# 32 of 256 tokens of an expert layer go by gathered rows on GpSimd and ScalarE instead of through the dense products

## The chip, the cores and the metric

One core of one Trainium2 chip. The metric is the device time of the kernel in microseconds (us), the median of several runs; lower is better.

## What is computed

A transformer layer of a hybrid kind on 256 tokens of width 1024, and then a second layer with other mixers, a cross attention and a feed-forward part. The change concerns the last part of the first layer, a lookup of experts:

```python
def peer_layer(h, w_q, keys, u, v):           # h: 256 tokens x 1024
    q = (h @ w_q).reshape(B, S, 8, 2, 128)
    ...
    # 8 heads x 16 = 128 experts (idx) and gates for each token, out of 16384
    def expert_block(args):
        ht, it, gt = args
        ue = jnp.take(u, it, axis=0)
        act = jax.nn.gelu(jnp.einsum('tkd,td->tk', ue, ht), approximate=False)
        ve = jnp.take(v, it, axis=0)
        return jnp.einsum('tk,tkd->td', gt * act, ve)
```

u and v are tables of 16384 rows of 1024 numbers, 64 MB each. All arithmetic is float32.

## The kernel before

The kernel doesn't gather. It multiplies every token with all 16384 rows of u, applies the gelu, multiplies the result by a gate that is zero for experts that the token didn't choose, and multiplies with all rows of v. Both tables are streamed once, as 128 units of 128x1024 floats each (512 KB), by the queue of SyncE (SP). The order of work is written out by hand for each engine; semaphores are the only link between them. The units of all weights of the kernel are numbered through, and the same steps are done for each unit i:

- SP: `fetch(i)` loads `raw[i % 4]` once the low part of unit i-4 is cut.
- ScalarE (ACT): `hi(i)` rounds the unit to float32r, `whi[i % 3]`, once TensorE (PE) has finished unit i-3.
- VectorE (DVE), or for some units GpSimd (POOL): `lo(i)` takes the rounded part from the raw one and so makes `wlo[i % 3]`. `on_pool` gives the choice: POOL for the first 62 or so units of u, DVE for the rest of u and all of v.
- PE: `three(...)` makes the product of both split operands in three float32r passes: high by high, high by low and low by high.

**Up-projection (u).** `lin_T`: for each unit 8 blocks of 128x128 weights, each with 3 matmuls whose moving operand is the 256 tokens of `hTh`/`hTl`: 24 matmuls of 128x256 for each unit. ACT evicts two units at a time with the gelu into `acts`, which holds 128 units by 256 tokens.

**Gates.** During the first 62 units DVE does the top-16 searches (`routing`) for both halves of the tokens. From unit 62 on, `gates` runs beside the units: for each group of 8 tokens and each half of the experts, DVE builds one-hot matrices (`oh`, `og_eq`, `og`, float16; three instructions with two operands in SBUF each), PE multiplies them (16 matmuls of 64 columns, L433 `bank<-og,oh`), and DVE multiplies the result into `acts` (`weigh`, L1715, one operand in PSUM). One group takes two steps, one step is made for each unit, and there are 64 groups: 33 of them during u and 31 during v.

**Down-projection (v).** For each unit, `cut_acts(n)` splits `acts` of the unit (ACT rounds, DVE subtracts), and PE makes 12 matmuls with 512 columns into four banks that are held for the whole of v. Later in v the norm of the `mem` input (`mem_norm`) and some loads of constants are put in.

`Side.step` moves the interleaved work on: each `yield` of a generator is one step.

Of the kernel before, what the change touches and what calls it, by code (L numbers as in the profile page):

```python
# [17 lines left out]
P = 128  # L18
# [15 lines left out]


# [28 lines left out]
    ("cfw", 66), ("cfb", 22),  # L64
# [53 lines left out]
def on_pool(i):  # L118

    slot = i - 2  # L120
    if BASE["u"] <= slot < BASE["u"] + 62:
# [34 lines left out]
own_act own_dve own_pool zeros x_sq hi_half lo_half lo_first f_xg f_xd f_act hd_mask  # L156
""".split()
# [39 lines left out]
def build(nc, x, mem, wdram, keep_d, con0_d, con1_d, con2_d, keys_d, w2c_d, gf_d, gf2_d, out):  # L197
    ctx = ExitStack()
    with ctx:
# [41 lines left out]
        s_raw = [sem(f"s_raw{i}") for i in range(NRAW)]  # L241
        s_in, s_in2, s_keep, s_con0, s_con1, s_con2, s_keys, s_w2c, s_gf, s_gf2, s_mem, s_out, s_w0, s_rest = (
# [103 lines left out]
        acts = t3(A2[:, :], P)  # L346
# [11 lines left out]
        assert 8192 + at0 + 2048 <= 256 * 61 and 8192 + at0 + 4096 <= 256 * 72  # L358
# [63 lines left out]
        def pe_program(e):  # L422
# [136 lines left out]
            def lin_T(u0, units, src, K, first=None, after=None, steps=(1,)):  # L559
# [215 lines left out]
            def gates(half):  # L775
                o1 = t4(oh1[:, :], OP, P)
                o2 = og[:, :].rearrange("p (m j i r) -> p m j i r", m=OP, j=2, r=2)
                for g in range(T // OB):
                    G = 32 * half + g
# [263 lines left out]
            lin_T(BASE["u"], 62, hTv, KD, steps=U1_STEPS)  # L1043
            side.drain()
            side.lists[0] += [gates(0), gates(1)]
            lin_T(BASE["u"] + 62, 66, hTv, KD)

            for i in range(4):
                use(i)
            for n in range(128):  # L1050
# [6 lines left out]
                for m in both:  # L1057
                    e.wait_ge(s["ca_lo"], m + 1)

# [19 lines left out]
                if n == 72:  # L1079
                    side.lists[0].append(mem_norm())  # L1080
# [67 lines left out]
        def act_program(e):  # L1148
# [176 lines left out]
            def cut_acts(n):  # L1325
                if n > 127:
                    return
                e.wait_ge(s["g_mul"], 32 if n < 64 else 64)
                if n >= 2:
                    e.wait_ge(s["w"], BASE["v"] + max(n - 7, 0))  # L1330
                act(cut(0, n), acts[:, n, :], ACT.Copy).then_inc(s["ca_hi"], 1)

            def mem_norm():
                e.wait_ge(s_mem, 32)
                e.wait_ge(s["ca_lo"], 72)
# [232 lines left out]
            def gelu(n0):  # L1568
                def f(n, pb):
                    if 256 * (n0 + n + 2) > 15872:  # L1570
                        e.wait_ge(s["rt_dve"], 8)
                    act(acts[:, n0 + n:n0 + n + 2, :], pb, ACT.Gelu).then_inc(s["ev_act"], 1)
# [5 lines left out]
            def first_cuts(u):  # L1578
                if u == 64:
                    cut_acts(0)  # L1580
                    cut_acts(1)

            lin_T(BASE["u"] + 62, 66, gelu(62), first_cuts)
            for n in range(128):
                hi(BASE["v"] + n + 2)
                if n == 62:
# [5 lines left out]
                if n == 72:  # L1592
# [105 lines left out]
        def dve_program(e):  # L1698
# [297 lines left out]
            def routing(b):  # L1996
# [62 lines left out]
                tt(g2[:, :, 1, :], gt, g2[:, :, 0, :], ALU.subtract).then_inc(s["rt_dve"], 1)  # L2059
                yield  # L2060

            def gates(half):
# [6 lines left out]
                def build(g):  # L2069
                    G, t = 32 * half + g, g * OB  # L2070
# [15 lines left out]
                def weigh(g):  # L2086
                    G, t = 32 * half + g, g * OB
# [6 lines left out]
                for g in range(T // OB):  # L2094
# [5 lines left out]
                weigh(T // OB - 1)  # L2100

            def cut_acts(n):
# [3 lines left out]
                tt(cut(1, n), acts[:, n, :], cut(0, n).bitcast(F32), ALU.subtract).then_inc(s["ca_lo"], 1)  # L2106
# [346 lines left out]
            lin_T(BASE["u"], 62, steps=U1_STEPS)  # L2453
            side.drain()
            side.lists[0] += [gates(0), gates(1)]
            lin_T(BASE["u"] + 62, 66)
            cut_acts(0)
            cut_acts(1)
            for n in range(128):
                lo(BASE["v"] + n + 2)  # L2460
                if n == 62:
                    side.drain()
                cut_acts(n + 2)
# [3 lines left out]
                if n == 72:  # L2467
# [79 lines left out]
        def pool_program(e):  # L2547
# [14 lines left out]

            def units(u0, n, steps=(1,)):
                for i in range(u0, u0 + n):
                    lo(i + 2)
                    side.step(steps[(i + 1) % len(steps)])
# [20 lines left out]
            own(e.memset(mhalf, -0.5))  # L2587
# [266 lines left out]
```

## Time and profile before

| what | value |
|---|---|
| device time, median of 3 runs (lowest, highest) | 1445.22 us (1444.06, 1445.54) |
| span of the profiled execution | 1441.8 us |
| own time of the profiled execution | not listed apart; the median of the runs is 3.4 us above the span |
| busy: PE, DVE, ACT, POOL | 99%, 67%, 51%, 15% of the span |
| TensorE's granted clock | full, in all 40 slices of the page |

How to read it: PE is the matmuls, PEld the loads of weights beside them, L433 is the line in which the helper `mm` emits each matmul, L1154, L1712 and L1715 are the helpers `act`, `tt` and `stt` of ACT and DVE. So an instruction is known by its tiles, not by its line. POOL is idle in most of the kernel and busy in the first half of u.

### The profile page before, as it was taken

To read this page: it belongs to the slowest core of one execution; us is meant where nothing else is said; L and a number is where in the kernel's file an instruction comes from. 1 tells how busy PE (TensorE), PEld (TensorE's weight loads), DVE (VectorE), ACT (ScalarE), POOL (GpSimd) and SP (SyncE) were. 2 spreads that over 40 slices of the span, in tenths; PEclk is the share of its full clock that TensorE was granted. 3 is DMA by queue.
4 is the path that set the end of the run, shared out by engine and by line. 5 is a ranking of instruction groups with operands and counts; after the bars stand their busy time and mean duration, and the time that the engine had idled before them with its cause. 6 is when DMAs were issued, how large, how long until landed. Compare 5 with 4: busy or idle time off the path is not lost.

```text
span 1441.8 us, 25221 instructions
## 1 busy us (share of the span) xinstructions
PE 1422.6 (99%) x10281; PEld 1290.2 (89%) x10281; DVE 967.4 (67%) x1752; ACT 738.5 (51%) x1066; POOL 212.7 (15%) x122
## 2 busy tenths in 40 slices
PE   8999999999999999999999999999999999999997
PEld 7989989999999999998777778888899788899986
DVE  5565674693944777778888876655577864677754
ACT  5674654545454444444444445544567754655543
POOL 5000000488883000000000000000114100000000
PEclk9999999999999999999999999999999999999999
DMA  6433456455555545445545466555543453455552
GB/s 241 142 132 125 138 157 216 141 186 180 187 180 182 170 162 174 164 164 173 174 164 174 164 222 245 181 185 188 175 147 118 159 177 112 154 188 185 181 190 103
DMA packets 67219, 245.07 MB, mean 170 GB/s; under 512 B 7456, under 2 KB 7712, under 8 KB 66848
## 3 DMA queue, kind: packets, MB, share of 16 engines
q1 hardware_dynamic: 66960, 243.19, 50.5%
q8 instruction: 82, 1.34, 0.4%
q14 instruction: 33, 0.27, 0.1%
q10 hardware_dynamic: 144, 0.26, 0.0%
HBM read 242.37 MB, written 1.05 MB: 169 GB/s over the span
## 4 chain that ended last, share of the span: by engine, by line
PE 77%; issue 14%; DVE 4%; ACT 4%; POOL 1%; DMA 0%; POOLq 0%; SPq 0%; DVEq 0%; ACTq 0%
PE bank L433 76%; ACT A L1154 2%; DVE wlo L1712 1%; ACT whi L1154 1%; PE bank L442 1%; DVE A L1712 1%; ACT L1154 1%; DVE A L1708 0%; DVE xres L1712 0%; DMA xres<-in_x 0%; POOL wlo L2555 0%; ACT hTh L1154 0%; DVE small L2361 0%; DVE small L1712 0%; POOL small L2561 0%
## 5 line engine op out<-in xcount | busy, mean ns | idle before, releaser
L1712 DVE TENSOR_TENSOR wlo<-raw,whi 128x1024 fp32r<-128x1024 f32 (+1 forms) x375 | 458.1, 1223 | 334.3 <-ACT whi L1154 333.9
L1154 ACT ACTIVATE whi<-raw 128x1024 fp32r<-128x1024 f32 (+1 forms) x450 | 472.9, 1053 | 401.3 <-PE bank L433 401.3
L433 PE MATMUL bank<-hTh,whi 128*128 128x256 f32 x1944 | 555.5, 286 | 2.0 <-DVE wlo L1712 1.3
L433 PE MATMUL bank<-hTl,whi 128*128 128x256 f32 x1944 | 548.6, 282 | 0.0
L433 PE MATMUL bank<-hTh,wlo 128*128 128x256 f32 x1944 | 548.0, 282 | 0.0
L433 PEld LDWEIGHTS bank<-hTh,whi 128*128 128x128 f32 x1944 | 367.0, 189 | 5.9 <-DVE wlo L1712 2.1
L433 PEld LDWEIGHTS bank<-hTh,wlo 128*128 128x128 f32 x1944 | 366.0, 188 | 0.0
L433 PEld LDWEIGHTS bank<-hTl,whi 128*128 128x128 f32 x1944 | 365.5, 188 | 0.3 <-issue 0.2
L433 PE MATMUL bank<-whi,hTh 128*128 128x512 f32 (+2 forms) x552 | 218.4, 396 | 0.2
L433 PE MATMUL bank<-wlo,hTh 128*128 128x512 f32 (+2 forms) x552 | 215.0, 390 | 0.0
L433 PE MATMUL bank<-whi,hTl 128*128 128x512 f32 (+2 forms) x552 | 214.9, 389 | 0.0
L2555 POOL TENSOR_TENSOR wlo<-raw,whi 128x1024 fp32r<-128x1024 f32 x73 | 175.2, 2401 | 267.6 <-ACT whi L1154 263.7
L1154 ACT ACTIVATE A<-bank 128x512 f32<-128x512 f32 (+2 forms) x163 | 90.7, 563 | 225.9 <-PE bank L433 216.2
L2561 POOL TENSOR_TENSOR small<-small 128x1 f32<-128x1 f32 x16 | 9.5, 593 | 935.9 <-DVE small L1709 932.1
L433 PEld LDWEIGHTS bank<-whi,hTl 128*128 128x128 f32 x552 | 104.0, 188 | 23.8
L433 PEld LDWEIGHTS bank<-whi,hTh 128*128 128x128 f32 x552 | 104.1, 189 | 23.4 <-DVE wlo L1712 0.8
L433 PEld LDWEIGHTS bank<-wlo,hTh 128*128 128x128 f32 x552 | 104.2, 189 | 22.2
L433 PE MATMUL bank<-A 128*128 128x128 f32 (+9 forms) x472 | 69.9, 305 | 0.0
L433 PEld LDWEIGHTS bank<-A 128*128 128x128 f32 (+4 forms) x472 | 59.5, 183 | 6.5 <-issue 2.5
L1712 DVE TENSOR_TENSOR hTl<-A,hTh 128x256 fp32r<-128x256 f32 x126 | 52.6, 418 | 0.5 <-ACT hTh L1154 0.5
L1154 ACT ACTIVATE hTh<-A 128x256 fp32r<-128x256 f32 x126 | 50.6, 401 | 1.9 <-DVE A L1715 1.9
L1715 DVE SCALAR_TENSOR_TENSOR A<-bank,A 128x512 f32<-128x512 f32 (+1 forms) x76 | 49.4, 658 | 2.3 <-PE bank L433 2.2
(178 smaller groups left out, 1391.8 us busy)
## 6 DMA issues: line engine op xcount, KB each, us to landing
raw<-in_u SPq DMA_DIRECT2D x128, 512.0 KB, 3.3
raw<-in_v SPq DMA_DIRECT2D x128, 512.0 KB, 3.3
raw<-in_w_up SPq DMA_DIRECT2D x44, 512.0 KB, 3.3
raw<-in_w_down SPq DMA_DIRECT2D x22, 512.0 KB, 3.2
raw<-in_w_in_t SPq DMA_DIRECT2D x17, 512.0 KB, 3.4
raw<-in_w_in_g SPq DMA_DIRECT2D x16, 512.0 KB, 3.3
raw<-in_w_out SPq DMA_DIRECT2D x16, 512.0 KB, 4.0
raw<-in_w_pq SPq DMA_DIRECT2D x16, 512.0 KB, 3.5
```

The lines of the kernel that those rows point to most:

```text
L433: return e.matmul(o, l, r, start=st, stop=sp_, skip_group_check=True)
L442: return e.transpose(o, i, ident[0:k, 0:k])
L1154: return e.activation(o, i, func, **kw)
L1712: return e.tensor_tensor(o, a, b, op)
L1715: return e.scalar_tensor_tensor(o, a, z, b, op0, op1, **kw)
L2555: e.tensor_tensor(l, raw[i % NRAW][:, :], h.bitcast(F32), ALU.subtract).then_inc(s["lo_pool"], 1)
L2561: e.tensor_tensor(st[:, 2:3], st[:, 3:4], mhalf, ALU.pow).then_inc(s["n_rstd"], 1)
```

## The change

The first 32 tokens leave the dense products. `acts` and the up-projection are made for 224 tokens (`c0=NG`): the matmuls of u have 224 columns instead of 256, the gates have 28 groups for each half instead of 32 and begin at unit 70 instead of 62, and the columns of these 32 tokens in the cut activations are set to zero by memsets. For the 32 tokens the 32x128 chosen rows are taken as 32 batches of 128 rows (4 slots of 32 tokens): POOL gathers them from u by indirect DMA (512 KB each, three buffers in the place that `acts` gives free), POOL multiplies them with the replicated tokens `hrep`, ACT sums along the row, and the gelu and the gate give 32 coefficients per partition. Then POOL gathers the rows of v, ACT scales them, POOL adds them up in `pk_acc`, and PE adds the four slots into the banks of v with two float32 matmuls before the last unit. Steps with DVE in them are the four `rep_h`, some small copies at the end of the first `routing`, and one product of 32 columns. The loads of `mem` and of constants and `mem_norm` move by 9 units, since `acts` ends elsewhere. One load of 512 KB (`hrep`) is added after `keys`.

```diff
+NG = 32
+NJ = P // NG
+NPK = P // NJ
+TD = T - NG
+NGRP = TD // OB
+NBUF = 3
+G_DENSE = 70
+REP_AT, GATHER_AT, MUL_AT, SUM_AT = 50, 60, 64, 65
+GATHER_V, SCALE_V, ACC_V = 40, 44, 45
+MEM_AT = 81
...
-                            ins = three(banks[bk][:, (n % 2) * 256:(n % 2 + 1) * 256], [z[:, j, k, :] for z in wv],
-                                        [z[:, k, :] for z in src], k == 0, k == K - 1)
+                            ins = three(banks[bk][:, (n % 2) * 256:(n % 2 + 1) * 256 - c0], [z[:, j, k, :] for z in wv],
+                                        [z[:, k, c0:T] for z in src], k == 0, k == K - 1)
...
-            lin_T(BASE["u"], 62, hTv, KD, steps=U1_STEPS)
+            lin_T(BASE["u"], 62, hTv, KD, steps=U1_STEPS, c0=NG)
             side.drain()
+            lin_T(BASE["u"] + 62, G_DENSE - 62, hTv, KD, c0=NG)
             side.lists[0] += [gates(0), gates(1)]
-            lin_T(BASE["u"] + 62, 66, hTv, KD)
+            lin_T(BASE["u"] + G_DENSE, P - G_DENSE, hTv, KD, c0=NG)
...
+                if m == 127:
+                    e.wait_ge(s["pk_used"], 2 * NPK)
+                    for h in range(2):
+                        mm(banks[h][0:NG, :], K_("pick"), pk_acc[:, h * 512:(h + 1) * 512], False, False)
...
+            def pick_sum(u):                      # ACT
+                g, r = divmod(u - SUM_AT, 2)
+                if r == 0 and 0 <= g < NPK:
+                    e.wait_ge(s["pk_mul"], g + 1)
+                    z = pk_buf(g)
+                    act(z, z, ACT.Copy, accum_out=pk_dot[:, g:g + 1]).then_inc(s["pk_used"], 1)
...
+                if r == 0 and 0 <= i < NPK:       # ACT, in v
+                    if i == 0:
+                        e.wait_ge(s["pk_co"], 1)
+                    e.wait_ge(*pk_landed(NPK + i))
+                    z = pk_buf(NPK + i)
+                    act(z, z, ACT.Copy, scale=pk_co[:, i:i + 1]).then_inc(s["pk_scaled"], 1)
...
+                stt(hrep[q, :], xres[0:NG, 0:D], small[0:NG, 2:3], hrep[q, :], ALU.mult, ALU.mult).then_inc(s["pk_rep"], 1)
...
+            def gather(g):                        # POOL
+                if g >= NBUF:
+                    e.wait_ge(s["pk_used"], g - NBUF + 1)
+                table, i = (utab, g) if g < NPK else (vtab, g - NPK)
+                e.indirect_dma_start(out=pk_buf(g), out_offset=None, in_=table,
+                                     in_offset=bass.IndirectOffsetOnAxis(ap=pk_idx[:, i:i + 1], axis=0)
+                                     ).then_inc(s_pick[g % NBUF], 16)
+
+            def picks(u):
+                g, r = divmod(u - GATHER_AT, 2)
+                if r == 0 and 0 <= g < NPK:
+                    gather(g)
+                g, r = divmod(u - MUL_AT, 2)
+                if r == 0 and 0 <= g < NPK:
+                    ...
+                    e.tensor_tensor(z, z, hrep, ALU.mult).then_inc(s["pk_mul"], 1)
+
+            def picks_v(n):
+                i, r = divmod(n - GATHER_V, 2)
+                if r == 0 and 0 <= i < NPK:
+                    gather(NPK + i)
+                i, r = divmod(n - ACC_V, 2)
+                if r == 0 and 0 <= i < NPK:
+                    e.wait_ge(s["pk_scaled"], i + 1)
+                    z = pk_buf(NPK + i)
+                    if i == 0:
+                        e.tensor_copy(pk_acc, z).then_inc(s["pk_used"], 1)
+                    else:
+                        e.wait_ge(s["pk_used"], NPK + i)
+                        e.tensor_tensor(pk_acc, z, pk_acc, ALU.add).then_inc(s["pk_used"], 1)
```

## Rows read from the trace of the kernel before

**Rows 1.** Page, head: the span.
```profile
span 1441.8 us, 25221 instructions
```
**Rows 2.** Chain that ended last, 440 to 1030 us, by line.
```profile
by line: PE bank L433 99.7%; PE bank L442 0.3%; issue 0.0%
```
**Rows 3.** Windows: length, busy us (count) by engine, clock, DMA share, GB/s.
```profile
455.00:645.00 190.00, 190.00 (x1923) 188.57 (x1923) 137.66 (x181) 78.26 (x91) 0.00 (x0) 1.00 0.51 167
660.00:840.00 180.00, 180.00 (x1167) 142.79 (x1167) 152.87 (x234) 79.30 (x116) 0.00 (x0) 1.00 0.51 170
```
**Rows 4.** Timeline of PE at 26 to 34 us: start, us, instruction.
```profile
25.96 0.22 PE L433 MATMUL bank<-whi,hTh 128*128 128x128 f32 x1
...
31.16 0.27 PE L433 MATMUL bank<-whi,hTl 128*128 128x128 f32 x1
...
31.43 0.28 PE L433 MATMUL bank<-hTl,whi 128*128 128x256 f32 x1
...
34.06 0.28 PE L433 MATMUL bank<-hTh,wlo 128*128 128x256 f32 x1
```
**Rows 5.** Timeline of the weight loads before 16 matmuls of 32 columns.
```profile
136.08 1.87 PEld L433 LDWEIGHTS bank<-A 128*128 128x128 f32 x16
```
**Rows 6.** Timeline around one pair of units of u with gates: DVE, ACT, PE.
```profile
625.46 0.68 DVE L1712 TENSOR_TENSOR oh<-iota_b,row_b 128x1024 f16<-128x1024 f16 x1
...
627.13 1.22 DVE L1712 TENSOR_TENSOR wlo<-raw,whi 128x1024 fp32r<-128x1024 f32 x1
630.05 1.22 DVE L1712 TENSOR_TENSOR wlo<-raw,whi 128x1024 fp32r<-128x1024 f32 x1 [1.71 <-ACT whi L1154]
631.20 0.68 DVE L1715 SCALAR_TENSOR_TENSOR A<-bank,A 128x512 f32<-128x512 f32 x1
631.80 0.68 DVE L1712 TENSOR_TENSOR oh<-iota_b,row_b 128x1024 f16<-128x1024 f16 x1
...
628.28 0.66 PE L433 MATMUL bank<-og,oh 128*128 128x64 f16 x16
...
628.48 0.60 ACT L1154 ACTIVATE A<-bank 128x512 f32<-128x512 f32 x1 [1.76 <-PE bank L433]
628.97 1.05 ACT L1154 ACTIVATE whi<-raw 128x1024 fp32r<-128x1024 f32 x1
```
**Rows 7.** Timeline of POOL and DVE where both are busy.
```profile
348.50 2.39 POOL L2555 TENSOR_TENSOR wlo<-raw,whi 128x1024 fp32r<-128x1024 f32 x1 [0.91 <-ACT whi L1154]
348.59 2.45 DVE L1712 TENSOR_TENSOR gate<-iT,gate 128x128 f16<-128x128 f32 x1
...
8.75 1.99 POOL L2592 TENSOR_TENSOR wlo<-raw,whi 128x512 fp32r<-128x512 f32 x1 [0.93 <-ACT whi L1154]
8.91 0.68 DVE L1712 TENSOR_TENSOR wlo<-raw,whi 128x512 fp32r<-128x512 f32 x1
```
**Rows 8.** Groups by line and form: busy us, mean ns of one.
```profile
L1712 DVE TENSOR_TENSOR A<-A 128x128 f32<-128x128 f32 x4 | 1.4, 345 | 0.1
L2596 POOL TENSOR_TENSOR wlo<-raw,whi 128x512 fp32r<-128x512 f32 x1 | 1.3, 1283 | 0.0
L2555 POOL TENSOR_TENSOR wlo<-raw,whi 128x1024 fp32r<-128x1024 f32 x73 | 175.2, 2401 | 267.6 <-ACT whi L1154 263.7 <-DVE A L1708 2.5
L1154 ACT ACTIVATION_READ_ACCUMULATOR A<-xres 128x1 f32 x26 | 4.9, 187 | 0.0
L433 PE MATMUL bank<-A 128*128 128x512 f32 x8 | 3.9, 592 | 0.0
L433 PE MATMUL bank<-A 128*128 128x256 f32 x80 | 18.6, 378 | 0.0
```
**Rows 9.** Timeline of DVE, one pair of units of v with gates.
```profile
770.51 1.22 DVE L1712 TENSOR_TENSOR wlo<-raw,whi 128x1024 fp32r<-128x1024 f32 x1
...
772.97 1.23 DVE L1712 TENSOR_TENSOR wlo<-raw,whi 128x1024 fp32r<-128x1024 f32 x1 [0.91 <-ACT whi L1154]
...
776.71 1.22 DVE L1712 TENSOR_TENSOR wlo<-raw,whi 128x1024 fp32r<-128x1024 f32 x1
```

More of the change, by code:

```diff
@@ L345, in build, with pk_buf, pk_landed @@
         sel_i = [scw[:, 0:128], scw[:, 128:256]]
-        acts = t3(A2[:, :], P)
+        acts = t3(A2[:, 0:P * TD], P)
+        hrep = a2(31744, 1024)
+        pk_acc = hrep
+        pk_idx = small[:, 16:16 + NPK].bitcast(U32)
+        pk_gate, pk_dot, pk_co, pk_f = (small[:, o:o + NPK] for o in (48, 80, 112, 144))
+        def pk_buf(g):
+            return a2(28672 + 1024 * (g % NBUF), 1024)
+        def pk_landed(g):
+            return s_pick[g % NBUF], 16 * (g // NBUF + 1)
         def cut(part, n):
@@ L557, in normed, with lin_T @@
                 return lambda k: e.wait_ge(s["n_lo"], 8 * j + 2 * (k // 2) + 2) if k % 2 == 0 else None
-            def lin_T(u0, units, src, K, first=None, after=None, steps=(1,)):
+            def lin_T(u0, units, src, K, first=None, after=None, steps=(1,), c0=0):
                 per = KD // K
@@ L777, in gates @@
                 o2 = og[:, :].rearrange("p (m j i r) -> p m j i r", m=OP, j=2, r=2)
-                for g in range(T // OB):
-                    G = 32 * half + g
+                for g in range(NGRP):
+                    G = NGRP * half + g
                     bk = gate_bank(half, g)
@@ L2059, in routing, with rep_h, pick_u, pick_v @@
                 tt(g2[:, :, 1, :], gt, g2[:, :, 0, :], ALU.subtract).then_inc(s["rt_dve"], 1)
-                yield
+                if b == 0:
+                    for j in range(NJ):
+                        q, z = slice(NG * j, NG * j + NG), slice(NPK * j, NPK * j + NPK)
+                        own(stt(pk_f[q, :], sel_i[1][0:NG, z], float(P), sel_i[0][0:NG, z], ALU.mult, ALU.add))
+                        own(e.tensor_copy(pk_gate[q, :], bex[0:NG, z]))
+                    again()
+                    e.tensor_copy(pk_idx, pk_f).then_inc(s["pk_idx"], 1)
+                yield
+            def rep_h(j):
+                q = slice(NG * j, NG * j + NG)
+                if j == 0:
+                    e.wait_ge(s_gffn, 16)
+                    e.wait_ge(s["r_add"], 4)
+                    e.wait_ge(s["n_rstd"], 3)
+                stt(hrep[q, :], xres[0:NG, 0:D], small[0:NG, 2:3], hrep[q, :], ALU.mult, ALU.mult).then_inc(s["pk_rep"], 1)
+            def pick_u(u):
+                if REP_AT <= u < REP_AT + 2 * NJ and (u - REP_AT) % 2 == 0:
+                    rep_h((u - REP_AT) // 2)
+            def pick_v(n):
+                if n == ACC_V - 4:
+                    e.wait_ge(s["pk_act"], 1)
+                    tt(pk_co, pk_co, pk_gate, ALU.mult).then_inc(s["pk_co"], 1)
             def gates(half):
@@ L2092, in weigh @@
                         ALU.mult, ALU.mult).then_inc(s["g_mul"], 1)
-                for g in range(T // OB):
+                for g in range(NGRP):
                     if g:
@@ L2105, in cut_acts @@
                 e.wait_ge(s["ca_hi"], n + 1)
-                tt(cut(1, n), acts[:, n, :], cut(0, n).bitcast(F32), ALU.subtract).then_inc(s["ca_lo"], 1)
+                if n == 2:
+                    for z in (hTh, hTl):
+                        own(e.memset(t3(z[:, :].bitcast(F32), 8)[:, :, 0:NG], 0.0))
+                    again()
+                tt(cut(1, n)[:, NG:T], acts[:, n, :], cut(0, n)[:, NG:T].bitcast(F32), ALU.subtract
+                   ).then_inc(s["ca_lo"], 1)
             def mem_norm():
```

82 lines of the change are left out of this document (57 added, 25 removed).

## The prediction, made before the changed kernel was run

> **What bounds the kernel now.** I read the chain of waits first: between 440 and 1030 us, which is most of u and all of v, it is matmuls for 99.7% [rows 2]. The windows confirm it: PE is busy for the whole of both stretches with gates, at a granted clock of 1.00, its 2.4 GHz level, while DVE has 138 of 190 us in u and 153 of 180 us in v, and POOL nothing [rows 3]. So before the change a matmul's time is the kernel's time there, and the reader is to see two things: DVE, the engine next to the limit, has 15 to 28% to spare, and POOL has everything. The change spends POOL's time to save PE's. The question is whether it really touches only these two.
>
> **What the columns save.** The timeline of PE has both widths in one stretch [rows 4]. From 31.43 to 34.06 there are 22 steps of matmuls with 256 columns: 2.63/22 = 119.5 ns each. From 25.96 to 31.16 there are 47 steps with 128 columns: 5.20/47 = 110.6 ns. Half the columns save 8.9 ns, not 53. What remains is the load of the next weights: sixteen loads ahead of matmuls of 32 columns take 1.87 us, 117 ns each [rows 5]. So 224 columns should go at this floor, 110.6 ns, and not at 119.5 x 224/256 = 104.6. I take 110.6; the saving is bounded by nothing and by the 32 columns' own time at 2.4 GHz, 13.3 ns. With 24 matmuls a unit it is 24 x 8.9 = 0.21 us, and 27 us over 128 units if PE stays the limit.
>
> The Trainium skill, page "TensorE: Matmul & The Clock Gate", sections "Back-to-back issue gap" and "LDWEIGHTS (loading the stationary operand)", gives N/2.4 + 2.5 ns for N columns, by which the full 13.3 ns would be saved, 41 us in all, and P/1.2 = 107 ns for a load of P = 128 columns, a floor near the measured one. The row decides for the floor, and so against a third of the hoped gain.
>
> **What the new work costs DVE.** Rows 7 carry the argument. At 348.59 DVE starts a product with two operands in SBUF, 128x128; such a one takes 345 ns in the mean [rows 8]. It took 2.45 us, and ended 0.15 us after the POOL instruction that had started 0.09 us before it. The reverse is at 8.75: POOL's 512-wide subtraction took 1.99 us where the same takes 1.28 [rows 8], and the 0.7 us between them is DVE's 0.68 us instruction. So a DVE instruction with two SBUF operands and a POOL instruction exclude each other for their whole length; one with an operand in PSUM runs freely. In the kernel before they hardly meet: POOL cuts in the first half of u, where DVE's searches have one operand or one in PSUM, and is idle after. Now POOL multiplies 128x1024, 2.40 us as its cuts [rows 8], once for each pair of units from unit 64 of u on, and adds as much from unit 45 of v to 107. DVE's `lo`, `oh`, `og_eq`, `og` all have two SBUF operands.
>
> **The pair of units in u with gates (units 70 to 127, 29 pairs).** Before: 6.34 us (631.80 - 625.46, [rows 6]), of which 48 x 0.1195 = 5.74 is matmuls and 0.60 the 16 of the gate group. If PE alone set it, it would now be 48 x 0.1106 + 0.60 = 5.91. But the next group's operands come by a chain. ACT evicts the unit (begins 0.20 us after PE is through, takes 0.50 to the next instruction), then cuts; DVE makes `lo` (630.05 to 631.20), `weigh` (0.60) and the three one-hot steps (1.67, from 625.46 to 627.13). From the start of the eviction at 628.48 to the end of `og` at 633.47 this is 4.99 us, 5.19 from PE's end, well under 6.34 [rows 6]. The change puts `pick_sum` between eviction and cut: 1.05 us [rows 6] and the read of the accumulator 0.19 [rows 8]: 6.43. And POOL's product, released by the sum before, falls on it: it is issued some 3.2 us after PE's end (0.2 + 0.5 + 1.25 and a gather's issue), waits for `lo` to finish near 4.1, holds the ports until 6.5, and `oh`, which wants them at 4.8, comes 1.7 us late. The chain is then 8.1 us. A group's operands are built from one pair before, so two periods make chain plus PE's 5.91: the pair takes (8.1 + 5.91)/2 = 7.0 us, unless DVE's own sum is longer: 6.34 less its 1.71 of idle is 4.6, with 1.7 to 2.3 of blocking 6.3 to 6.9. So 7.0, and 7.0 - 6.34 = +0.69 a pair. If the whole 2.3 blocks, 7.3; with no blocking, 6.17.
>
> The issue of a gather isn't in the trace. Its bounds are nothing and one full POOL instruction, 2.4 us [rows 8]; I take the middle, 1.2. POOL's own loop for a pair (sum 1.25, issue, wait for `lo` up to 1.1, product 2.4) is 6 us, under 7.0, and at the upper end 7.2. The Trainium skill, page "DMA: Bandwidth & Descriptors", section "Latency and other measured facts", gives about 1 us for the first byte of a DMA issued from GpSimd, which would leave the sum as it is. The 64 gathers add 32 MB: half a unit for each unit, beside a DMA share of 0.51 [rows 3], at most 0.77, with three buffers ahead; nothing.
>
> **The sum.**
> - Units 0 to 69 of u, POOL or DVE cutting, no product in the way or few: 70 x 0.214 = -15.0.
> - Eight gate groups of 64 fall away, 4 before unit 70 and 4 in v: 8 x 0.60 = -4.8.
> - 29 pairs: +20.0 (no blocking -4.9; full +28.4).
> - v, units 45 to 54, 5 pairs with gates and additions. The pair is 6.20 us, DVE idle in 0.91 of it [rows 9]: 5.29 + 1.7 to 2.3 = 7.0 to 7.6, +0.8 to +1.4 each, +5 (0 if nothing blocks).
> - v, units 55 to 107: of the 5.29 of DVE the gates' 2.27 are gone, 3.0 remain, with 2.3 it is 5.3, under PE's 6.20 - 0.60 = 5.6: nothing. In the some 16 units with `mem_norm` it is over: +2 (0 to 6). If PE's cover were gone, the cost would be the 5.3.
> - `rep_h`: 4 DVE products, 1.22 each, against POOL's cuts at 2.40 in a unit that is now 2.65, which regain 0.25 a unit; and some nine small copies after `routing(0)`, each up to 2.4 late, against DVE's spare time before the transposes: +3 (0 to 8).
> - The two float32 matmuls of 512 columns before the last unit, four records of 3.9/8 = 0.49 [rows 8]: +2. Memsets, the wait before v, the load of `hrep`: +1 (0 to 3).
>
> Together +13.2 us. The profiled span of 1441.8 [rows 1] becomes 1455; with the 3.4 us that the median of the runs lies above it, 1445.2 + 13 = **1458**. The likeliest case's own range is from blocking of 1.0 us (pair 6.66, 1446) to all upper ends (pair 7.3, +5 to +7 for v, 8, 6, 3), 1480.
>
> **The rivals.**
> 1. *The ports are not held, or hit idle time: faster.* DVE is idle 1.71 us before `lo` [rows 6]. If POOL's product fell there, or ACT's chain alone remained, the pair would be 6.17: -15.0 - 4.8 - 4.9 + 3 to 5 for the rest = -20, 1425. It decides where the blocking for each pair is under 0.8 us, since 29 x 0.46 = 13. Against it: the product is released by the sum and so comes just after `lo` begins, every time. Chance 0.27.
> 2. *The gather's issue holds the ports too, or is long.* Another 1.2 us in the chain is +0.6 x 29 = +17, and in v DVE goes from 5.3 to 6.5 against 5.6, +0.9 x 31 = +28: 1503. Nothing in the trace speaks on it, as POOL issues no DMA. Chance 0.10. The Trainium skill, page "SBUF — State Buffer", section "SBUF: two separate sides", has VectorE and GpSimd share a pair of ports under an exclusive lock for a whole instruction, which agrees with [rows 7], but counts a VectorE operation with two SBUF inputs as a holder only against GpSimd work that reads SBUF; descriptors are written there, so by it this rival falls away and the 1458 stands.
> 3. *Below 256 columns a float32r matmul goes at half rate.* 128 columns in 110.6 ns would still allow it (2 x 128 / 2.4 = 107), and the engine has such a rate: a float32 record of 256 columns lasts 378 ns [rows 8] where float32r has 280 [rows 4]. It would be 187 + 12 ns, 3072 x 79 = +240: 1690. Against it, the first 128-column matmul, not queued behind a load, took 0.22 us [rows 4]. Chance 0.02.
> 4. *No change*: losses between cases 1 and the main one that cancel 20 us of gain. Chance 0.05.
>
> The rest, 0.56, is the forecast.
>
> **How the numbers follow.** A run of this kernel tells a change of 0.2%, 3 us, from none. Faster: nearly all of rival 1, 0.26. Same: rival 4, and the edges of rival 1 and the forecast, 0.08. Slower: 0.66. The range must hold case 1 down to its own price and the forecast, and part of rival 2: 1424 to 1495; outside are rival 3, the upper half of rival 2 and the lower edge of rival 1, with unknown sizes 0.2 in all.
>
> **What would show it.** 224-column matmuls 110 to 111 ns apart in units 0 to 60; if 104 to 106, the floor was wrong and 4 to 5 us more per 1000 matmuls are gained; if near 200, rival 3. In u from 70 on, `og` or `oh` at 0.68 us in the mean under rival 1, and with one of each pair's two-operand instructions at 2 us or more here, PE idle behind `og`, the pair 7.0 us apart. POOL's products at 2.4 us with a DVE wait in front that makes them up to 3.5. In v after 55, PE without idle. If ACT's `pick_sum` waits for POOL by 1 us or more in each pair, the gather's issue is the bound instead.

## The result, and the profile after

The changed kernel takes 1490.7 us (median of 4 runs, 1488.4 to 1491.3) where the kernel before takes 1445.1 beside it: a ratio of 1.0315, with a 95% interval of 1.0301 to 1.0330, so it is slower by 45.6 us. 1458.0 was predicted, with a range of 1424 to 1495 and 0.66 for slower. The direction was right; of the loss less than a third was foreseen.

Where the time lies is read from marks that both timelines have: ACT's evictions of unit pair 0, of pair 34 (units 68 and 69, the last before gates in the new kernel) and of pair 63 (the last of u), and the first matmul after v.

| stretch | before | after | difference | predicted |
|---|---|---|---|---|
| pair 0 to pair 34 (34 pairs, to unit 69) | 198.2 | 184.7 | -13.5 | -15.0 - 2.4 + 3 = -14.4 |
| pair 34 to 63 (29 pairs with gates) | 183.6, 6.33 each | 236.7, 8.16 each | +53.1 | +20.0 |
| pair 63 to the end of v | 380.4 | 390.5 | +10.1 | -2.4 + 5 + 2 + 2 + 1 = +7.6 |
| the rest of the span | 679.6 | 677.3 | -2.3 | 0 |

One row is far off, the second. The head of the page and the windows of the changed kernel, which answer to [rows 1, 3]:

```profile
span 1489.2 us, 25201 instructions
...
PEclk9999999999999999998999999999999999999999
...
455.00:645.00 190.00, 156.33 (x1505) 152.63 (x1505) 165.99 (x140) 85.52 (x120) 81.53 (x48) 0.93 0.62 199
660.00:840.00 180.00, 171.15 (x1179) 140.55 (x1179) 149.34 (x217) 79.21 (x119) 15.22 (x10) 0.97 0.54 176
```

PE, busy in all 190 us before, is now idle in 34 of them, and a second thing has changed that was nowhere in the prediction: the granted clock is 0.93. Who keeps PE waiting stands in the waits of PE (waited for, total, times, longest):

```profile
PE bank L459 <- DVE og L1763: 47.0, 23, 7.4
PE bank L459 <- DVE wlo L1763: 6.1, 12, 1.8
```

That is the predicted place, the chain that builds `og`. The width did what it should. The timeline of PE, a little behind a gate group:

```profile
552.09 0.28 PE L459 MATMUL bank<-hTh,whi 128*128 128x224 f32 x1
...
556.11 0.28 PE L459 MATMUL bank<-hTh,whi 128*128 128x224 f32 x1
```

From 552.09 to 556.11 there are 36 matmuls: 4.02/36 = 111.7 ns, the forecast floor of 110.6 within 1%, and not 104.6.

Now the pair with gates, to be laid beside [rows 6]. The timeline of ACT, DVE, POOL and PE in the changed kernel, where the pair's last matmul ends near 567.6:

```profile
567.61 0.66 PE L459 MATMUL bank<-og,oh 128*128 128x64 f16 x16
...
569.65 0.98 POOL L2656 DMA_INDIRECT A<-in_utab,small  x1 [7.10 <-ACT A L1186]
570.66 2.41 POOL L2670 TENSOR_TENSOR A<-A 128x1024 f32<-128x1024 f32 x1
...
570.37 3.79 DVE L1763 TENSOR_TENSOR wlo<-raw,whi 128x1024 fp32r<-128x1024 f32 x1 [2.19 <-ACT whi L1186]
574.08 0.68 DVE L1766 SCALAR_TENSOR_TENSOR A<-bank,A 128x512 f32<-128x512 f32 x1
574.68 0.68 DVE L1763 TENSOR_TENSOR oh<-iota_b,row_b 128x1024 f16<-128x1024 f16 x1
...
575.73 0.69 DVE L1763 TENSOR_TENSOR og<-og_eq,gate 128x1024 f16<-128x1024 f16 x1
...
576.48 0.65 PE L459 MATMUL bank<-og,oh 128*128 128x64 f16 x16 [2.78 <-DVE og L1763]
```

`lo` is asked for at 570.37 and POOL's product begins only at 570.66, yet `lo` takes 3.79 us instead of 1.22: it comes 2.57 us late, more than the product's whole length, and ends 1.1 us after the product. I had it the other way round: `lo` first, the product waiting, and `oh` 1.7 us late. `oh` takes its normal 0.68. The product, which I had down for up to 3.5 us, takes 2.41.

The second surprise is what PE does after the wait. Its timeline after another of these, at 560.05:

```profile
560.05 0.65 PE L459 MATMUL bank<-og,oh 128*128 128x64 f16 x16 [2.77 <-DVE og L1763]
...
560.84 0.41 PE L459 MATMUL bank<-hTh,wlo 128*128 128x224 f32 x1
...
563.82 0.41 PE L459 MATMUL bank<-hTl,whi 128*128 128x224 f32 x1
564.03 0.38 PE L459 MATMUL bank<-hTh,wlo 128*128 128x224 f32 x1
```

The 14 steps from 560.84 to 563.82 are 213 ns each, not 111: after 2.77 us of idle PE runs at its 1.2 GHz level for some 3.4 us, and so loses 16 x 0.1 = 1.6 us more (1.3 behind the wait that ends at 543.66). Such a wait comes with every second gate group; the group between has none (567.61) or a short one of 0.46. But not each of them is followed by the lower level. Of the 13 waits of 2.1 to 2.8 us from 463.82 to 656.3, nine are, with 11 to 16 steps near 213 ns, and four of 2.8 are not. The timeline of PE after one of these four:

```profile
480.24 0.66 PE L459 MATMUL bank<-og,oh 128*128 128x64 f16 x16 [2.77 <-DVE og L1763]
...
481.03 0.27 PE L459 MATMUL bank<-hTh,wlo 128*128 128x224 f32 x1
...
483.37 0.27 PE L459 MATMUL bank<-hTh,wlo 128*128 128x224 f32 x1
```

These 21 steps are 2.34/21 = 111 ns each.

The third is at the end of u. With no more gathers to issue, three products stand one behind the other on POOL (DVE, then POOL, then PE):

```profile
666.59 8.39 DVE L1763 TENSOR_TENSOR wlo<-raw,whi 128x1024 fp32r<-128x1024 f32 x1 [2.50 <-ACT whi L1186]
...
666.87 7.01 POOL L2670 TENSOR_TENSOR A<-A 128x1024 f32<-128x1024 f32 x3
...
677.30 1.03 PE L459 MATMUL bank<-og,oh 128*128 128x64 f16 x16 [7.38 <-DVE og L1763]
```

One `lo` comes 7.2 us late, behind all three, and PE waits 7.4.

### The profile page after: what moved, and what is told of

Its sections match the earlier page's. It is cut to its first block, busy times and chain, and to the rows that moved or that the text cites. A ratio compares the mean times of both kernels' runs of the same rounds, so it can differ in the third digit from the quotient of the medians.

```text
span 1489.2 us, 25201 instructions
## 1 busy us (share of the span) xinstructions
PE 1413.4 (95%) x10156; PEld 1275.5 (86%) x10157; DVE 1108.7 (74%) x1738; ACT 797.9 (54%) x1163; POOL 455.6 (31%) x250
## 4 chain that ended last, share of the span: by engine, by line
PE 63%; issue 19%; DVE 9%; ACT 7%; POOL 1%; DMA 0%; POOLq 0%; SPq 0%; ACTq 0%; DVEq 0%
PE bank L459 62%; DVE wlo L1763 3%; ACT A L1186 3%; ACT whi L1186 2%; POOL wlo L2641 1%; DVE A L1759 1%; PE bank L468 1%; DVE og L1763 1%; DVE A L1766 1%; DVE oh L1763 1%; DVE A L1763 1%; ACT L1186 1%; DVE og_eq L1763 0%; DVE xres L1763 0%; DMA xres<-in_x 0%
## 5 line engine op out<-in xcount | busy, mean ns | idle before, releaser
L1763 DVE TENSOR_TENSOR wlo<-raw,whi 128x1024 fp32r<-128x1024 f32 (+1 forms) x375 | 548.8, 1468 | 262.3 <-ACT whi L1186 261.7
L459 PE MATMUL bank<-hTh,whi 128*128 128x224 f32 (+1 forms) x1944 | 555.7, 286 | 4.7 <-DVE wlo L1763 3.7
L459 PE MATMUL bank<-hTl,whi 128*128 128x224 f32 (+1 forms) x1944 | 547.2, 282 | 0.0
L459 PE MATMUL bank<-hTh,wlo 128*128 128x224 f32 (+1 forms) x1944 | 547.2, 281 | 0.0
L459 PEld LDWEIGHTS bank<-hTl,whi 128*128 128x128 f32 x1944 | 377.4, 194 | 0.3 <-issue 0.2
L1186 ACT ACTIVATE A<-bank 128x512 f32<-128x512 f32 (+3 forms) x163 | 87.2, 542 | 210.9 <-PE bank L459 201.3
L1763 DVE TENSOR_TENSOR hTl<-A,hTh 128x224 fp32r<-128x224 f32 x126 | 96.0, 762 | 2.2
L2684 POOL TENSOR_TENSOR A<-A 128x1024 f32<-128x1024 f32 x31 | 76.3, 2462 | 50.0 <-ACT A L1186 49.9
L459 PE MATMUL bank<-og,oh 128*128 128x64 f16 x896 | 37.9, 196 | 47.0 <-DVE og L1763 47.0
L459 PEld LDWEIGHTS bank<-og,oh 128*128 128x128 f16 x896 | 31.0, 99 | 58.8 <-DVE og L1763 52.5
L2670 POOL TENSOR_TENSOR A<-A 128x1024 f32<-128x1024 f32 x32 | 76.9, 2406 | 0.7
```

Source lines behind the costliest of these rows:

```text
L459: return e.matmul(o, l, r, start=st, stop=sp_, skip_group_check=True)
L1186: return e.activation(o, i, func, **kw)
L1763: return e.tensor_tensor(o, a, b, op)
L2670: e.tensor_tensor(z, z, hrep, ALU.mult).then_inc(s["pk_mul"], 1)
L2684: e.tensor_tensor(pk_acc, z, pk_acc, ALU.add).then_inc(s["pk_used"], 1)
```

## The experiments

Theory: VectorE (DVE) and GpSimd (POOL) exclude each other ("the ports" stands for what only one of them holds at a time), the product hits `lo` because of where the gather's issue puts it, and the clock adds to each wait. Rivals: the gather's issue itself holds the ports; ScalarE's sum in the chain; the mere amount of POOL's work. "Pair" is the mean period of the 29 pairs with gates, 8.16 us in the changed kernel and 6.33 before. The batches of runs were taken apart: the kernel before had medians of 1443.8 to 1445.1 us in them, so a difference of 1 us between two experiments says nothing.

**The ports (e1_tiny_products).** The products and additions have 8 columns, so their results are left out except for these; gathers, sums and every wait stay.

```diff
-                    e.tensor_tensor(z, z, hrep, ALU.mult)...
+                    e.tensor_tensor(z[:, 0:8], z[:, 0:8], hrep[:, 0:8], ALU.mult)...
-                        e.tensor_tensor(pk_acc, z, pk_acc, ALU.add)...
+                        e.tensor_tensor(pk_acc[:, 0:8], z[:, 0:8], pk_acc[:, 0:8], ALU.add)...
```

> The changed kernel with POOL's products and additions made on 8 of the 1024 columns (so the picked tokens' sums are incomplete); gathers, ACT's sums and scalings and every wait stay. Theory (a POOL product and a DVE instruction with two SBUF operands exclude each other, and that delay lies in the chain to the gate matmuls): the pair of units from unit 70 of u falls from 8.16 us to between 6.0 and 6.4, v loses its 8 us, together 1425 to 1440 us. Rival (ACT's sum ahead of its cut makes the chain too long by itself): the pair stays above 7.5, about 1480. Rival (the gathers' issue or their traffic): above 1475.

Measured: 1419.4 us, ratio 0.9828 [0.9812, 0.9845], pair 6.09 us, as the theory had it; the whole is 6 us under the 1425 expected at least. So some 71 of the 1491 us hang on the length of POOL's products and additions. The timeline of DVE and POOL in this kernel settles rival 2 of the prediction as well:

```profile
546.75 1.23 DVE L1763 TENSOR_TENSOR wlo<-raw,whi 128x1024 fp32r<-128x1024 f32 x1 [1.32 <-ACT whi L1186]
...
546.04 0.98 POOL L2656 DMA_INDIRECT A<-in_utab,small  x1 [3.95 <-ACT A L1186]
547.04 0.99 POOL L2670 TENSOR_TENSOR A<-A 128x8 f32<-128x8 f32 x1
```

`lo` is asked for in the middle of the issue, as in the changed kernel, and takes its normal 1.23. The issue doesn't keep DVE out at this point.

**No picked work at all (e4_dense_only).** Gathers, products, sums, scalings, additions, `rep_h` and the final matmuls are left out, so the 32 tokens get nothing from this layer's experts.

```diff
             def picks(u):
+                return
...
             def picks_v(n):
+                return
...
             def pick_sum(u):
+                return
```

> The changed kernel with nothing of the picked rows but the indices and the load of the replicated gain: no gathers, products, sums, additions, and no two matmuls for them (the 32 tokens get nothing from the experts). This is the most that the 224 columns and the 56 gate groups can give. Expected: 3072 matmuls at 111.5 ns instead of 119.5 and 8 groups at 0.6 us, 25 + 5 less, 1414 to 1420 us. If the columns gave their full share of 13.3 ns, 1400; if PE ran into DVE anyway, 1430 or more.

Measured: 1409.3 us, 0.9755 [0.9739, 0.9771], pair 5.91, as worked out in the prediction for PE alone. The whole is 5 us under the 1414 to 1420 expected. The kernel before took 1443.9 us beside it, so this is what the dense side saves: 34.6 us, the most that the change could bring. All of it and 46 us more go into the picked side.

**Without the gathers (e2_three_gathers).** Only the first three gathers are issued, and the waits for the others are met by these; later products work on what lies in the buffers, so the output of the 32 tokens is not theirs. Products, sums and additions stay, and ACT's scalings wait for a free buffer in the gathers' place.

```diff
                 if g >= NBUF:
                     e.wait_ge(s["pk_used"], g - NBUF + 1)
+                    return
```

> The changed kernel with only the first three of 64 gathers (the products run on the same three buffers again and again, the picked tokens' results are wrong); products, sums, scalings, additions and waits for free buffers stay. Theory of the ports: the product then starts right behind the sum, while ACT cuts, and still delays DVE's cut, by 1.6 to 1.7 us instead of 2.6: pair 7.0 to 7.5 us, 1462 to 1475 us in all. Rival (issue, traffic or landing of the gathers is the cost): the pair at 6.4 or less, 1435 or less.

Measured: 1453.4 us, 1.0064 [1.0047, 1.0081], pair 6.95, under what was expected on both counts. The gathers, which harm nobody by themselves (e1), cost 35 us of the pairs' time (29 x (8.16 - 6.95)), the clock's part included. That it is the place of their issue, and not their traffic, e7 shows below, which has all of them. The timeline of e2 shows how:

```profile
549.96 2.56 DVE L1764 TENSOR_TENSOR wlo<-raw,whi 128x1024 fp32r<-128x1024 f32 x1 [0.86 <-ACT whi L1186]
...
549.05 2.39 POOL L2672 TENSOR_TENSOR A<-A 128x1024 f32<-128x1024 f32 x1 [4.44 <-ACT A L1186]
```

Without the issue in front, the product begins 0.9 us ahead of `lo` instead of 0.3 behind it, and `lo` comes 1.34 us late and not 2.57. The issue delays the product into the worst place of those seen here.

**Without ScalarE's sum (e3_tiny_sum).** The sum reads 8 columns, so the coefficients are wrong sums.

```diff
-                    act(z, z, ACT.Copy, accum_out=pk_dot[:, g:g + 1])...
+                    act(z[:, 0:8], z[:, 0:8], ACT.Copy, accum_out=pk_dot[:, g:g + 1])...
```

> The changed kernel with ACT's sum over 8 of the 1024 columns (the picked tokens' dot products are incomplete). Theory of the ports: 0.9 us leave the chain that two periods share, and the product still hits DVE's cut: the pair 7.6 to 7.8 us, 1473 to 1482 us. Rival (ACT's sum in the chain is the cost): the pair at 6.4, 1435 to 1445.

Measured: 1465.3 us (1456.5 to 1473.8, a spread that no other kernel shows), 1.0152 [1.0096, 1.0207], pair 7.28. More than expected comes back, 25 us, but `lo` still takes 3.86 us at 558.21, and in some pairs `oh` 2.29. The sum in the chain is a part of the cost, not the main one, and the 25 us hold a part of the clock's, which is at 0.98 in 455 to 645 for 0.93; how the meeting point wanders from run to run I haven't followed up.

**The clock (e9_filled_stalls).** Eight matmuls of zeros ahead of every second gate group, into the bank that this group then overwrites. Nothing is left out.

```diff
-                    e.wait_ge(s["g_og"], G + 1)
                     use(bk)
+                    if G % 2 == 0 and G < 28:
+                        spin(8, bk)
+                    e.wait_ge(s["g_og"], G + 1)
```

> Eight matmuls of zeros (512 columns, 1.7 us) ahead of every second gate group of u, the one before which TensorE waits 2.1 to 2.8 us; they write into the group's own bank, which the group then overwrites. Nothing that VectorE, ScalarE or GpSimd do is changed. If the fall to the 1.2 GHz level after each wait costs what the pitch says (12 to 18 matmuls at 213 instead of 111 ns, 1.3 us in two pairs), the granted clock of this stretch stays at 1.00, the pair goes from 8.16 to 7.5 us and the time to 1470 to 1475. Rival: the clock's fall lies in time that the chain would have needed anyway: 1488 to 1492.

Measured: 1474.1 us, 1.0207 [1.0190, 1.0224], pair 7.59. More work on PE makes the kernel 16.6 us faster. The windows of this kernel, to be read against the first window after the change (0.93):

```profile
455.00:645.00 190.00, 178.21 (x1735) 160.28 (x1734) 173.79 (x153) 92.56 (x130) 96.66 (x52) 1.00 0.64 215
```

`lo` is blocked as before (3.77 us at 546.08). So 16.6 us of the 53.1 are the clock alone: 236.7 to 220.1 for the 29 pairs. A count gives the same: the changed kernel has some 155 steps near 213 ns there, 0.10 us too long each. In the regular part of this kernel four pairs take 29.6 us, 7.4 each.

**The width (e5_256_columns).** The changed kernel with matmuls of 256 columns in u; the first 32 are computed and not used.

```diff
-            lin_T(BASE["u"], 62, hTv, KD, steps=U1_STEPS, c0=NG)
+            lin_T(BASE["u"], 62, hTv, KD, steps=U1_STEPS)
...
-                    act(acts[:, n0 + n:n0 + n + 2, :], pb[:, :, 0:TD], ACT.Gelu)
+                    act(acts[:, n0 + n:n0 + n + 2, :], pb[:, :, NG:T], ACT.Gelu)
```

> The changed kernel with up-projection matmuls of 256 columns again (only the last 224 are evicted). If dropping 32 columns saves what I predicted, 8 to 9 ns a matmul down to the 111 ns floor, this costs 24 x 8 to 9 = 0.20 us a unit in units 0 to 69, +14 us, and half of it or less in the pairs after, where the chain shares the period: +3 to +6. Together 1506 to 1512, matmul pitch 119.5. Rival: narrower matmuls save nothing and the gain of units 0 to 69 came from elsewhere: 1490.

Measured: 1502.7 us, 1.0404 [1.0387, 1.0422]. The columns do save, 12 us, less than expected. Pair 0 to 34 takes 194.8 us for 184.7: 10.1/68 = 0.149 us a unit where 0.214 was raw. With 256 columns it is 194.8/(34 x 48) = 119.4 ns a matmul, the full old pitch; with 224 it is 113.2, not 111. The 3 us between are in part the picked work: without it (e4) the stretch takes 182.9 us. PE is busy for 178.8 of 180 us from 270 on, and for 180.0 with 256 columns, so wider matmuls hide these small waits again. In the pairs with gates it is 8.22 for 8.16: there the columns are worth almost nothing.

**Where the product falls.** Four kernels compute all that the changed kernel does and only place things differently.

e6_product_after_lo: the product waits for the low part of the odd unit, the sum is one pair later, the gather's issue stands behind the product.

```diff
-REP_AT, GATHER_AT, MUL_AT, SUM_AT = 50, 60, 64, 65
+REP_AT, GATHER_AT, MUL_AT, SUM_AT = 50, 60, 64, 67
...
+                    e.wait_ge(*map(lambda q: s[q] if isinstance(q, str) else q, LOW[BASE["u"] + MUL_AT + 2 * g + 3]))
                     z = pk_buf(g)
                     e.tensor_tensor(z, z, hrep, ALU.mult)...
+                g, r = divmod(u - GATHER_AT, 2)      # moved here
```

> GpSimd's product waits until VectorE has made the low part of the odd unit, so that it falls into VectorE's idle time ahead of the next low part, and the sum comes one pair later; the same work in another place. If the loss is a matter of where the product meets VectorE's chain, the pair goes from 8.16 to 6.4 to 7.0 us (VectorE's own 3.9 us with two SBUF operands and the product's 2.4 are 6.3, the lower bound) and the time is 1440 to 1457. Rival: the loss is ScalarE's 1.25 us in the chain and the mere quantity of port time; then the pair stays near 8 and the time at 1485 to 1490.

e7_product_first: only product and issue change places, and the product takes over the issue's wait for the sum.

```diff
-                g, r = divmod(u - GATHER_AT, 2)
-                if r == 0 and 0 <= g < NPK:
-                    gather(g)
...
+                    if g:
+                        e.wait_ge(s["pk_used"], g)
                     e.wait_ge(*pk_landed(g))
                     z = pk_buf(g)
                     e.tensor_tensor(z, z, hrep, ALU.mult)...
+                g, r = divmod(u - GATHER_AT, 2)
+                if r == 0 and 0 <= g < NPK:
+                    gather(g)
```

> Product and gather issue change places: the product is released by the sum as before, and the issue stands behind it. Theory: the product wins over VectorE's low part because it stands directly behind the issue on GpSimd and VectorE asks while the issue runs. Then here the product starts 0.98 us earlier, the low part asks some 0.7 us after its start and comes 1.6 us late instead of 2.6: chain 7.9, pair 7.4 to 7.7; the last three products no longer run in one piece either (5 us): 1466 to 1478. If the issue behind the product keeps VectorE out too, the low part stays 2.6 us late and only the 5 us of the end come back: 1485.

Measured: e6 1458.4 us, 1.0101 [1.0084, 1.0117], pair 6.96, inside the 6.4 to 7.0 expected, and the whole just over the 1457 expected at most, with v at 395.0 us for 390.5. e7 1451.5 us, 1.0046 [1.0030, 1.0063], pair 6.79, far better than expected (7.4 to 7.7). I had left out what the clock gives back, 0.57 us a pair in e9; it is at 1.00 here, with waits of 0.64 to 0.77 us. Its timeline (DVE, POOL):

```profile
550.60 2.58 DVE L1763 TENSOR_TENSOR wlo<-raw,whi 128x1024 fp32r<-128x1024 f32 x1 [0.86 <-ACT whi L1186]
...
549.70 2.39 POOL L2669 TENSOR_TENSOR A<-A 128x1024 f32<-128x1024 f32 x1 [2.50 <-ACT A L1186]
552.24 1.79 POOL L2656 DMA_INDIRECT A<-in_utab,small  x1 [0.15 <-issue]
```

`lo` is 1.36 us late, as in e2, and the issue, now in no one's way, waits for `lo` itself (1.79 for 0.98). Moving two instructions past each other takes away 39 of the 45.6 us of loss, the clock's part and the three products in one piece included.

e8_paced_tail: only the last two products wait for the sum before theirs.

```diff
+                    if g > NPK - 3:
+                        e.wait_ge(s["pk_used"], g)
```

> Only the last two products wait for the sum before theirs. In the changed kernel no gather stands between the last three products, they run in one piece of 7.0 us, and VectorE's low part, asked for 0.3 us before the first of them, takes 8.4 us and TensorE waits 7.4 us. Theory: GpSimd's instructions standing back to back keep VectorE out, and this costs about 5 us once: 1485 to 1487. Rival: this wait is the end of the gates' first half, not the products: 1489 to 1491.

Measured: 1486.8 us, 1.0303 [1.0289, 1.0318], span 1485.0 for 1489.2. The interval overlaps that of the changed kernel, so by times alone this isn't shown. PE's longest wait falls from 7.4 to 4.8 us, and another of 1.6 comes behind it. Of the span's 4.2 us less, 1.4 lie ahead of pair 0, where the edit changes nothing; 1.4 lie in the 29 pairs and 1.5 in v. So what pacing gives is at most some 3 us, once.

e10_four_pieces: each product as four instructions of 256 columns.

```diff
-                    e.tensor_tensor(z, z, hrep, ALU.mult)...
+                    for q in range(4):
+                        ins = e.tensor_tensor(z[:, q * 256:(q + 1) * 256], z[:, q * 256:(q + 1) * 256],
+                                              hrep[:, q * 256:(q + 1) * 256], ALU.mult)
```

> Each product as four instructions of 256 columns. If GpSimd keeps the ports as long as its next instruction stands ready, the low part still comes 2.6 us late, or more by the pieces' own overhead, and the time is 1490 to 1500. Rival: VectorE gets in at every end of an instruction; then the low part waits for one piece (0.6 us), the later pieces fall on the fused product in PSUM and partly on the one-hot steps, the pair goes to about 7.2 and the time to 1462 to 1470.

Measured: 1470.3 us, 1.0183 [1.0169, 1.0197], pair 7.50, at the upper edge of the rival (1462 to 1470). My theory, that POOL keeps the ports as long as its next instruction stands ready, falls. The timeline of DVE and POOL:

```profile
541.23 1.45 DVE L1763 TENSOR_TENSOR wlo<-raw,whi 128x1024 fp32r<-128x1024 f32 x1 [1.08 <-ACT whi L1186]
...
543.81 0.96 DVE L1763 TENSOR_TENSOR og_eq<-iota_b,col_b 128x512 f16<-128x512 f16 x1
544.80 1.10 DVE L1763 TENSOR_TENSOR og<-og_eq,gate 128x1024 f16<-128x1024 f16 x1
...
541.52 4.96 POOL L2671 TENSOR_TENSOR A<-A 128x256 f32<-128x256 f32 x4
```

`lo`, asked for 0.29 us before the first piece, as it was before the whole product, is only 0.23 late here, and DVE gets in between the pieces. The four take 4.96 us for 2.4, and now ACT's sum waits for them 1.3 us in each pair.

**A version built on this.** e11_sum_after_cut: ScalarE cuts the unit first and sums after it; the product waits for the low part of that same unit, so that it meets the weighing (one operand in PSUM) and only then `oh`.

```diff
-REP_AT, GATHER_AT, MUL_AT, SUM_AT = 50, 60, 64, 65
+REP_AT, GATHER_AT, MUL_AT, SUM_AT = 50, 60, 64, 66
...
+                    if g:
+                        e.wait_ge(s["pk_used"], g)
+                    by, n = LOW[BASE["u"] + MUL_AT + 2 * g + 2]
+                    e.wait_ge(s[by], n)
                     e.wait_ge(*pk_landed(g))
```

(and the gather behind the product, as in e7).

> ScalarE sums after it has cut the unit, not before, and the product waits for VectorE's low part of that same unit; the gather's issue stands behind the product. Chain from the end of TensorE's pair: 0.7 for the eviction, cut 1.05, low part 1.15, then the product of 2.4 beside the 0.6 of the weighing, so that the one-hot steps come 1.8 us late, and their 1.67: 6.9 us. Pair (6.9 + 5.9)/2 = 6.4, VectorE's own sum gives the same: 1437 to 1443, so faster than the kernel before if slightly. Rival: what counts is the port time alone and its place doesn't matter beyond the version with product first (pair 6.79): 1449 to 1453.

Measured: 1445.7 us, 1.0007 [0.9998, 1.0017]: no difference to the kernel before, and 3 us or more over the 1437 to 1443 expected. It is the median of 11 runs, the lowest 1443.1; one of them took 5760 us, whose cause I don't know, and without it the median is 1445.3. Pair 6.52 for the expected 6.4. DVE and POOL:

```profile
547.10 0.68 DVE L1766 SCALAR_TENSOR_TENSOR A<-bank,A 128x512 f32<-128x512 f32 x1
547.70 2.57 DVE L1763 TENSOR_TENSOR oh<-iota_b,row_b 128x1024 f16<-128x1024 f16 x1
...
547.31 2.40 POOL L2671 TENSOR_TENSOR A<-A 128x1024 f32<-128x1024 f32 x1 [2.86 <-ACT A L1186]
```

The weighing runs beside the product at its normal 0.68, `oh` is 1.9 us late (2.57 for 0.68). That is the late `oh` that I had predicted for the changed kernel, made true by another order.

e12_norm_later: e11, and `mem_norm` begins 25 units later, when the additions are through.

```diff
-MEM_AT = 81
+MEM_AT = 106
```

> The kernel with the sum after the cut, and besides the norm of mem begins at step 106 of v instead of 81, when the additions are through. In the changed kernel its VectorE steps take 6.2 us for four where they met additions, and ten units with it took 35.1 us against 28.0 without and 29.9 before. Theory: 5 us less than the kernel it is built on. Rival: the norm then ends too late for what follows v, or the additions weren't the cause: no difference or slower.

Measured: 1437.7 us (1436.0 to 1439.6), 0.9956 [0.9943, 0.9970]. From pair 63 to the end of v it takes 387.3 us for 392.5, and the spans are 1435.9 and 1441.3, so the 5 us were there; the result computes all that the changed kernel does and is faster than both: by 6 us than before, 53 than the change as made. In the changed kernel the collision looks so (DVE, then POOL, then PE):

```profile
962.90 2.50 DVE L1759 TENSOR_SCALAR A<-A,small 128x256 f32<-128x256 f32 x1 [0.67 <-POOL small L2647]
...
970.44 4.10 DVE L1763 TENSOR_TENSOR wlo<-raw,whi 128x1024 fp32r<-128x1024 f32 x1
...
962.83 2.41 POOL L2684 TENSOR_TENSOR A<-A 128x1024 f32<-128x1024 f32 x1
...
970.66 0.77 PE L459 MATMUL bank<-whi,hTh 128*128 128x512 f32 x1 [3.65 <-DVE hTl L1763]
```

The instruction at 962.90 has one tensor operand and one value for each partition, all in SBUF, and takes 0.35 us in the mean where no addition runs (e12, after 850). Here it takes 2.50 beside an addition of 2.41. So it isn't only instructions with two tensors in SBUF that POOL keeps out.

## Why the prediction was right in direction and wrong in size

**What failed: the term "29 pairs: +20.0".** It measured +53.1, and it accounts for all of the error; the other terms together were off by 1 us. (By its own formula it should have read +19.3: (8.1 + 5.91)/2 - 6.34 is 0.67, not 0.69.) The step in it: "waits for `lo` to finish near 4.1, holds the ports until 6.5, and `oh`, which wants them at 4.8, comes 1.7 us late. The chain is then 8.1 us." Three things took its place:

- The order of the two. Product and `lo` are wanted within 0.3 us of each other, and I let `lo` win since it was asked for first. The product wins and `lo` is 2.57 us late. So it goes in the 25 products before which `lo` was asked for 0.24 to 0.43 us; in four more `lo` had been asked for 0.95 us ahead, and there it is the next `lo` that comes 2.2 late. The chain is (570.37 - 567.6) + 3.79 + what follows = 8.9 us (567.6 to 576.48) instead of 8.1, and by the same formula, (8.9 + 5.91)/2 = 7.4 for 7.0, +0.4 x 29 = +11 us. The kernel in which the clock is held (e9) has these 7.4. I had given a full block of 2.3 us as the upper bound, 7.3 a pair; the bound was nearer than the value taken. That the place decides, and not the amount of work, e2, e7 and e11 show: the same product in the changed kernel, 0.9 us earlier, and behind the low part gives 8.16, 6.79 and 6.52 (with the clock held, as it is in the other two, the first is 7.59).
- The clock. The prediction read 1.00 before and kept PE at 2.4 GHz in a stretch for which it forecast waits. It costs 16.6 us, shown by e9.
- The last three products in one piece: 7.4 us of PE's wait for the usual 2.8, +4.6. This one is argued from the wait; e8 gets back at most some 3 us, within the noise of the times. I had costed the pairs as if all were alike and never looked at what paces POOL when the gathers are out.

Together some 32 of the 33 us that were missed, of which the first two, 28, are shown.

The range of 1424 to 1495 held 1490.7 only by the share given to rival 2; the main case's own range ended at 1480.

**Units 0 to 69: the size was forecast.** Measured -13.5 for -14.4, in which two small misses cancel: without the picked work (e4) it is -15.3 where -17.4 was forecast, and the picked work costs 1.8 for 3. The floor of the pitch, from a 128-column stretch of another part of the kernel [rows 4], held for 224 columns (111.7 ns). By the Trainium skill, page "TensorE: Matmul & The Clock Gate", section "Back-to-back issue gap", N/2.4 + 2.5, it would be 95.8; the trace doesn't agree, as the row had said. The section itself gives this as the gap of an isolated matmul and has the pitch of a stream set by load and matmul together; the prediction used it without this.

**v.** Forecast +7.6, measured +10.1. Four gate pairs with additions, which answer to [rows 9], take 7.36 us for 6.20, and these were given 7.0 to 7.6; one `lo` of each is 2.2 late:

```profile
859.42 3.44 DVE L1763 TENSOR_TENSOR wlo<-raw,whi 128x1024 fp32r<-128x1024 f32 x1
...
859.37 2.41 POOL L2684 TENSOR_TENSOR A<-A 128x1024 f32<-128x1024 f32 x1 [3.04 <-ACT A L1186]
```

From 55 on PE doesn't wait for the additions, as forecast, but for once beside `mem_norm` (3.65 us at 970.66): the cut of `hTl` is blocked and covered. `mem_norm` was put at +2 with bounds of 0 to 6 and costs 5.3 (e11 to e12). The two float32 matmuls measure 1.88 us for the +2, in the changed kernel:

```profile
1075.34 1.88 PE L459 MATMUL bank<-A,keep 128*32 128x512 f32 x4 [0.18 <-issue]
```

**The rivals.** 1, ports not held: falls with e1 and every blocked `lo`; its number, 1425, is nearly what one gets when the products are gone (1419). 2, the issue holds the ports or is long: in u it takes 0.98 us in the middle of my bounds, and DVE runs beside it (e1). Yet its number, 1503, was nearer than mine. That is luck: the issue does its harm in u by pushing the product, and the 28 us that the rival had in v didn't come. Nor is the issue free of the ports: in v 25 issues that begin while VectorE is in a `lo` take 1.64 to 1.95 us. The rule of the Trainium skill, page "SBUF — State Buffer", section "SBUF: two separate sides", by which I let it fall, says who shares the ports and for how long, and the runs agree as to the products. It also says that whichever starts first gets them; that is how I ordered the two, and by the records it doesn't hold here, since `lo` starts at 570.37 and the product at 570.66, and the product goes first, if these starts, 0.29 us apart, are recorded rightly. 3, half rate: 111.7 ns excludes it. 4, no change: not for the change as made; e11 is such a kernel.

## What to carry to other kernels

Where two engines exclude each other, the price of an instruction is set by what it meets, not by its length: draw the meeting on a time axis, take the loss of the whole length for either side where the two are wanted within a few tenths of a microsecond, and look for an order in which the long one lies beside work that needs no shared port. A wait that is put on a TensorE that never waited can cost more than its length, as nine of 13 waits of 2.1 to 2.8 us did here: look at the granted clock once you forecast idle time, and give the matmuls after it a price at the lower level as the upper bound. And ask what paces a queue at its end: a producer that was held back by its loads runs free when these are out.

## What the runs showed of the hardware that I had not expected

- A GpSimd instruction of 128x1024 that began 0.3 us after VectorE's had been asked for (570.66 and 570.37) went first, in all 25 such meetings of u; one of 128x256 in the same place (e10) or of 128x8 (e1) did not: `lo` took 1.45 and 1.23 us. Three of 128x1024 in a row let VectorE in nowhere (8.39 us), four of 128x256 did. What the chip decides by is open; only lengths of 8, 256 and 1024 were tried.
- Nine of 13 idle times of 2.1 to 2.8 us on TensorE brought 11 to 16 matmuls near 213 ns, the other four none; of eight idle times of 1.7 us in e3 two brought 15. What separates them I haven't worked out. Idle times of 0.3 to 1.3 us in the regular pairs of e7, e10 and e11 left the granted clock of the stretch at 0.99 to 1.00.
- The issue of a gather of 128 rows of 4 KB occupies GpSimd for 0.94 to 1.21 us where VectorE leaves it alone, mostly 0.98, for 1.25 to 1.27 where it begins in an `oh` (e11), and for 1.64 to 1.97 in most cases where it begins in a `lo` (1.79 at 552.24 in e7).
